# A three-block network on one core: the third block's tail on 516 tokens in two halves of 258 columns, each laid at 192 modulo 256 bytes

## The reference

```
def third_block(x, meta_tokens, ...):
    h = concatenate([meta, x], axis=1)                  # 16 + 512 tokens
    h = h + hybrid_mixer(rms_norm(h, norm_mix_w), w_in, ...)
    h = h + conv_ffn_3(rms_norm(h, norm_ffn_w), ffn_w_up, conv_w, conv_b, ffn_w_down)
    return rms_norm(h, norm_final_w)[:, N_META:]

def hybrid_mixer(h, ...):
    proj = h @ w_in
    fox_qkv, fox_f, gdn_qkv, gdn_z, gdn_b, gdn_a, gates = split(proj)
    o_fox = forgetting_attention(...)                   # looks back over all tokens
    gdn_qkv = silu(causal_dwconv(gdn_qkv, gdn_conv_w))  # width 4
    o_gdn = gated_delta_rule(...)                       # a scan over all tokens
    o_gdn = rms_norm(o_gdn, gdn_norm_w) * silu(gdn_z)
    return (g_fox * (o_fox @ w_branch_fox) + g_gdn * (o_gdn @ w_branch_gdn)) @ w_out

def conv_ffn_3(h, ...):
    u = causal_dwconv(h @ w_up, conv_w, conv_b)         # width 3: needs two tokens ahead
    gate, up = u[..., :2816], u[..., 2816:]
    return (silu(gate) * up) @ w_down
```

## Time and profile before

| what | value |
|---|---|
| median of 3 runs | 2911.84 us (2908.43 to 2922.6) |
| profiled execution | 2912.08 us, of which the span is 2910.7 us |
| mean granted TensorE clock | 0.975 |
| PE, DVE, ACT, POOL busy | 95%, 55%, 36%, 21% |
| stages behind the scans | about 2278 to 2911 us of the span |

### The profile page before, as it was taken

One profiled execution on the slowest core, in us unless ns is written; L12 is line 12 of the kernel. 1 busy time (PEld: TensorE's weight loads), 2 busy tenths in 40 slices (PEclk: granted clock), 3 DMA queues, 4 the chain that ended last, 5 costly groups with the idle time before them and its releaser, 6 DMA issues. The chain is left out here.

```text
span 2910.7 us, 42543 instructions
## 1 busy us (share of the span) xinstructions
PE 2778.8 (95%) x16646; PEld 2344.9 (81%) x16646; DVE 1604.3 (55%) x2432; ACT 1047.3 (36%) x1786; POOL 616.8 (21%) x495
## 2 busy tenths in 40 slices
PE   8989999999999999999999999999898998999998
PEld 6769876888888767757788888976787998999986
DVE  5875566366643475934533337964443455666643
ACT  4354343432223323252423224546343333422223
POOL 3430110121100222440100003445453000111101
PEclk9999899999999999989999999998999999999999
DMA  4200321123233312202232222210000122222221
GB/s 158 91 6 8 102 87 59 58 90 99 94 97 99 111 61 74 87 10 85 90 100 94 94 96 72 89 37 1 6 2 1 59 88 80 80 92 91 87 97 63
DMA packets 60307, 210.62 MB, mean 72 GB/s; under 512 B 7926, under 2 KB 8566, under 8 KB 59990
## 3 DMA queue, kind: packets, MB, share of 16 engines
q1 hardware_dynamic: 58934, 207.39, 21.8%
q10 hardware_dynamic: 1184, 0.59, 0.1%
HBM read 205.84 MB, written 2.10 MB: 71 GB/s over the span
## 5 line engine op out<-in xcount | busy, mean ns | idle before, releaser
L278 PE MATMUL ps<-normed,slab_hi 128*128 128x264 f32 (+2 forms) x2568 | 871.0, 339 | 27.4 <-DVE normed L601 13.8
L280 PE MATMUL ps<-normed,slab_lo 128*128 128x264 f32 (+2 forms) x2568 | 849.0, 331 | 0.0
L279 PE MATMUL ps<-normed,slab_hi 128*128 128x264 f32 (+2 forms) x2568 | 847.9, 330 | 0.0
L159 ACT ACTIVATE slab_hi<-ring 128x1024 fp32r<-128x1024 f32 x376 | 397.0, 1057 | 953.9 <-PE ps L280 949.6
L163 DVE TENSOR_TENSOR slab_lo<-ring,slab_hi 128x1024 fp32r<-128x1024 f32 x360 | 480.2, 1336 | 381.1 <-ACT slab_hi L159 380.6
L278 PEld LDWEIGHTS ps<-normed,slab_hi 128*128 128x128 f32 x2568 | 485.3, 189 | 89.4 <-issue 33.8
L279 PEld LDWEIGHTS ps<-normed,slab_hi 128*128 128x128 f32 x2568 | 488.1, 190 | 47.0 <-issue 4.3
L280 PEld LDWEIGHTS ps<-normed,slab_lo 128*128 128x128 f32 x2568 | 485.3, 189 | 46.6
L278 PE MATMUL ps<-hidden,slab_hi 128*128 128x512 f32 x560 | 221.9, 396 | 5.6 <-DVE hidden L229 5.6
L280 PE MATMUL ps<-hidden,slab_lo 128*128 128x512 f32 x560 | 220.1, 393 | 0.0
L279 PE MATMUL ps<-hidden,slab_hi 128*128 128x512 f32 x560 | 219.4, 392 | 0.0
(11 more groups left out here) (579 smaller groups left out, 3942.1 us busy)
## 6 DMA issues: line engine op xcount, KB each, us to landing
ring<-in_stream SPq DMA_DIRECT2D x376, 512.0 KB, 3.3
h<-in_x SPq DMA_DIRECT2D x8, 256.0 KB, 5.5
mix_y<-in_sgu_b SPq DMA_DIRECT2D x1, 1024.0 KB, 6.1
out_features<-ffn_hidden SPq DMA_DIRECT2D x2, 512.0 KB, 3.2
xn<-in_c_recip_count SPq DMA_DIRECT2D x1, 512.0 KB, 3.4
rwkv_a<-in_mem SPq DMA_DIRECT2D x1, 512.0 KB, 3.9
rwkv_b<-in_mem SPq DMA_DIRECT2D x1, 512.0 KB, 5.0
sgu_ln<-in_sgu_ln SPq DMA_DIRECT2D x1, 512.0 KB, 6.8
```

The costliest lines, as they stand in the source:

```text
L159: self.nc.scalar.activation(self.hi[:, n % PARTS, :], self.ring[:, n % SLOTS, :], ACT.Copy).then_inc(self.hi_ready, 1)
L278: nc.tensor.matmul(to, lhsT[0], rhs[0], start=start, stop=False)
L279: nc.tensor.matmul(to, lhsT[0], rhs[1], start=False, stop=False)
L280: return nc.tensor.matmul(to, lhsT[1], rhs[0], start=False, stop=stop)
```

## The change

It has four parts. Nothing is computed otherwise than before; tokens 0 to 11 are no longer carried behind the scans.

1. Behind the scans the stages work on tokens 12 to 527 (`FROM = META - 4`, `TAIL = 516`), in two halves of 258 columns: gates, z, the norm of `yg`, the merge, the output projection, the norm of the feed-forward and its up-projection. The projections before the scans keep 528.
2. Moving operands of these stages are laid by halves: each half of a row has a space of `HALF = 320` words (1280 bytes, a multiple of 256) of its own, and begins at 192 modulo 256 bytes. `Rows` has a flag `apart` and `Rows.moving` for it, and the splits write a row as two pieces of 258.
3. The projections' rows (`CarriedRows`) are contiguous: 528 words are 2112 bytes, so the first row begins at 160 (`CARRIED_AT`), the next 64 bytes further modulo 256, and each second half 32 bytes beyond its first.
4. The feed-forward's buffer `ffn3_raw` is the norm's `square` buffer. The down-projection's operands still begin at 192.

The order of the instructions and their number stay the same on every engine; their sizes change. The diff, cut to its core (left out: the same change of `0:T3` to `FROM:T3` in the activations of the gates, `HALVES` to `TAIL_HALVES` in the merge and the output, and the shift of the convolution's columns by 12):

```diff
+FROM = META - 4
+TAIL = T3 - FROM
+TAIL_HALVES = [(FROM, FROM + TAIL // 2), (FROM + TAIL // 2, T3)]
...
-OPERAND_AT = 192
-WIDE_AT, WIDE = 224, 576
-HIDDEN_AT = (OPERAND_AT - WIDE_AT) % BOUNDARY // 4
+OPERAND_AT, CARRIED_AT = 192, 160
+HALF = 320
...
-        self.hi, self.lo = at or K.moving(ctx, "rows", [parts] + shape)
+        self.hi, self.lo = at or K.moving(ctx, "rows", [parts] + shape, HALF if len(shape) == 3 else 0)
...
     def slab(self, i):
...
-    def moving(self, ctx, name, shape):
-        at, pitch = (OPERAND_AT, shape[-1]) if shape[-1] <= S else (WIDE_AT, WIDE)
+    def moving(self, ctx, name, shape, pitch=0, at=OPERAND_AT):
+        pitch = pitch or shape[-1]
...
 def laid(space, shape, pitch):
...
-    return rows if len(shape) == 2 else rows.rearrange("p (a b) n -> p a b n", b=shape[1])
+    if len(shape) == 3:
+        return rows.rearrange("p (a b) n -> p a b n", b=shape[1])
+    return rows if len(shape) == 2 else rows.rearrange("p (a b c) n -> p a b c n", b=shape[1], c=shape[2])
...
 def load_stage(K, ins):
...
-    def __init__(self, K, ctx, gain, n, scale=None, known=False, arrived=None, src=None, like=None):
+    def __init__(self, K, ctx, gain, n, scale=None, known=False, arrived=None, src=None, like=None, apart=False, at=OPERAND_AT):
...
-            self.square, self.total, self.rstd = like.square, like.total, like.rstd
+            self.square, self.total, self.rstd, self.apart = like.square, like.total, like.rstd, like.apart
...
-        self.hi, self.lo = K.moving(ctx, "normed", [KT, n])
+        self.apart = apart
+        self.hi, self.lo = K.moving(ctx, "normed", [KT, 2, n // 2], HALF) if apart else K.moving(ctx, "normed", [KT, n], at=at)
...
+    def moving(self, k, c, lo, hi):
+        return [x[:, k, c] if self.apart else x[:, k, lo:hi] for x in (self.hi, self.lo)]
+    def shaped(self, x):
+        return x.rearrange("p (c n) -> p c n", c=2) if self.apart else x
     def split_hi(self, act, k):
...
-        self.K.nc.scalar.activation(self.hi[:, k], self.src(k), ACT.Copy, scale=self.K.vec(self.gain, k)).then_inc(self.hi_ready, 1)
+        self.K.nc.scalar.activation(self.hi[:, k], self.shaped(self.src(k)), ACT.Copy, scale=self.K.vec(self.gain, k)).then_inc(self.hi_ready, 1)
...
     def split_lo(self, dve, k):
...
-        self.K.nc.vector.scalar_tensor_tensor(out=self.lo[:, k], in0=self.src(k), scalar=self.K.vec(self.gain, k),
+        self.K.nc.vector.scalar_tensor_tensor(out=self.lo[:, k], in0=self.shaped(self.src(k)), scalar=self.K.vec(self.gain, k),
...
     def take_square(self, act, k):
...
     def __init__(self, K, ctx, scale, gains):
-        super().__init__(K, ctx, "norm_mix_w_3", T3, scale)
+        super().__init__(K, ctx, "norm_mix_w_3", T3, scale, at=CARRIED_AT)
...
-                           (rows.hi[:, k, lo:hi], rows.lo[:, k, lo:hi]), k == 0, k == KT - 1)
+                           rows.moving(k, c, lo, hi), k == 0, k == KT - 1)
...
 def half_product(K, feed):
...
     def product(i, b, start, stop):
-        lo, hi = HALVES[b % 2]
...
-            mm = exact(K.nc, K.ps[:, b, 0:hi - lo], cut(feed.slab(i), at, at + P), [x[:, k, lo:hi] for x in feed.acts(i)],
+            mm = exact(K.nc, K.ps[:, b, 0:TAIL // 2], cut(feed.slab(i), at, at + P), [x[:, k, b % 2] for x in feed.acts(i)],
...
-def pairs_of(x):
-    n = x.shape[1] // 2
-    return lambda i: x[:, 2 * (i % n):2 * (i % n) + 2, :]
+def tail_pair(x, i):
+    return x[:, 2 * i:2 * i + 2, FROM:T3].rearrange("p k (c n) -> p k c n", c=2)
...
 class Rates:
...
-        rows = Rows(K, local, "norm_mix_w_3", T3, scale, known=True)
+        rows = Rows(K, local, "norm_mix_w_3", TAIL, scale[:, FROM:T3], known=True, src=lambda k: K.h[:, k, FROM:T3], apart=True)
...
-        raw = K.buf(local, "gates3_raw", [P, 2, T3])
-        root = K.buf(local, "gdn_root_mean", [P, 4, T3])
+        raw = K.buf(local, "gates3_raw", [P, 2, TAIL])
+        root = K.buf(local, "gdn_root_mean", [P, 4, TAIL])
...
-                        nc.vector.tensor_scalar(cols.grid(root[:, t, :]), K.ps[:, 6:8, 0:T3 // 2], 1.0 / HD, EPS, ALU.mult, ALU.add).then_inc(mean_out, 1)
+                        nc.vector.tensor_scalar(cols.grid(root[:, t, :]), K.ps[:, 6:8, 0:TAIL // 2], 1.0 / HD, EPS, ALU.mult, ALU.add).then_inc(mean_out, 1)
...
-                    nc.gpsimd.tensor_tensor(root[:, t, :], yg[:, t, :], yg[:, t, :], ALU.mult).then_inc(squared, 1)
+                    nc.gpsimd.tensor_tensor(root[:, t, :], yg[:, t, FROM:T3], yg[:, t, FROM:T3], ALU.mult).then_inc(squared, 1)
...
-                    nc.gpsimd.tensor_tensor(yg[:, t, :], yg[:, t, :], z[:, t, :], ALU.mult)
+                    nc.gpsimd.tensor_tensor(yg[:, t, FROM:T3], yg[:, t, FROM:T3], z[:, t, FROM:T3], ALU.mult)
...
-        part = K.buf(local, "merge3_part", [P, 2, 8, T3 // 2])
-        feed = Feed(K, local, 8, lambda i: (yf, yg)[(i // 2) % 2][:, 2 * (i % 2):2 * (i % 2) + 2, :], [2, T3])
+        part = K.buf(local, "merge3_part", [P, 2, 8, TAIL // 2])
+        feed = Feed(K, local, 8, lambda i: tail_pair((yf, yg)[(i // 2) % 2], i % 2), [2, 2, TAIL // 2])
...
-            (lo, hi), at = HALVES[b % 2], merged(4 * (g // 2) + b // 2)
+            (lo, hi), at = TAIL_HALVES[b % 2], merged(4 * (g // 2) + b // 2)
...
     def __init__(self, K, x, then, parts):
...
-        self.feed = Feed(K, None, 8, pairs_of(x), [2, T3], parts=PARTS, at=parts)
+        self.feed = Feed(K, None, 8, lambda i: tail_pair(x, i % 4), [2, 2, TAIL // 2], parts=PARTS, at=parts)
...
-        spaces = K.spaces(local, "rows", WIDE_AT, PARTS * 2 * WIDE)
-        out3 = Residual3(K, K.xn, rows, [laid(x, [PARTS, 2, T3], WIDE) for x in spaces])
-        ffn = Ffn(K, local, "ffn3", rows, 2 * FT, FT, [laid(x, [PARTS, HIDDEN_AT + S], 2 * WIDE)[:, :, HIDDEN_AT:] for x in spaces])
-        raw = K.buf(local, "ffn3_raw", [P, 2, T3])
+        spaces = K.spaces(local, "rows", OPERAND_AT, PARTS * 4 * HALF)
+        out3 = Residual3(K, K.xn, rows, [laid(x, [PARTS, 2, 2, TAIL // 2], HALF) for x in spaces])
+        ffn = Ffn(K, local, "ffn3", rows, 2 * FT, FT, [laid(x, [PARTS, S], 4 * HALF) for x in spaces])
+        raw = rows.square
...
-                    link(nc.vector.tensor_scalar(to, x[:, META - 2:T3 - 2], K.vec("ffn_conv_w_3", w), K.vec("ffn_conv_b_3", w), ALU.mult, ALU.add))
+                    link(nc.vector.tensor_scalar(to, x[:, 2:2 + S], K.vec("ffn_conv_w_3", w), K.vec("ffn_conv_b_3", w), ALU.mult, ALU.add))
...
-        rows = Rows(K, span, "norm_ffn_w_3", T3)
+        rows = Rows(K, span, "norm_ffn_w_3", TAIL, src=lambda k: K.h[:, k, FROM:T3], apart=True)
```

More of the change, by code:

```diff
@@ L3372, in _ @@
                     if i < 4:
-                        nc.scalar.activation(z[:, i, :], raw[:, i % 2, :], ACT.Silu).then_inc(gated, 1)
+                        nc.scalar.activation(z[:, i, FROM:T3], raw[:, i % 2, :], ACT.Silu).then_inc(gated, 1)
                     else:
-                        nc.scalar.activation(gates[:, i - 4, :], raw[:, i % 2, :], ACT.Sigmoid, bias=K.vec("gate_bias_3", i - 4)).then_inc(gated, 1)
+                        nc.scalar.activation(gates[:, i - 4, FROM:T3], raw[:, i % 2, :], ACT.Sigmoid, bias=K.vec("gate_bias_3", i - 4)).then_inc(gated, 1)
                     if i == SUMS + 4:
@@ L3397, in _ @@
                         dve.wait_ge(inverted, i - APPLY + 1)
-                        at = yg[:, t, lo:hi]
+                        at = yg[:, t, FROM + lo:FROM + hi]
                         nc.vector.scalar_tensor_tensor(out=at, in0=at, scalar=gain, in1=root[:, t, lo:hi], op0=ALU.mult, op1=ALU.mult).then_inc(normed, 1)
@@ L3896, in _ @@
                     for b in range(8):
-                        (lo, hi), m = HALVES[b % 2], 4 * (g // 2) + b // 2
+                        (lo, hi), m = TAIL_HALVES[b % 2], 4 * (g // 2) + b // 2
                         group.bank_ready(dve, b)
@@ L3955, in vector @@
             for b in range(8):
-                (lo, hi), m = HALVES[b % 2], 4 * g + b // 2
+                (lo, hi), m = TAIL_HALVES[b % 2], 4 * g + b // 2
                 group.bank_ready(dve, b)
@@ L4101, in _ @@
                         dve.wait_ge(multiplied if o else silu, f - 1)
-                    link(nc.vector.tensor_scalar(to, x[:, META - 2:T3 - 2], K.vec("ffn_conv_w_3", w), K.vec("ffn_conv_b_3", w), ALU.mult, ALU.add))
-                    link(nc.vector.scalar_tensor_tensor(out=to, in0=x[:, META - 1:T3 - 1], scalar=K.vec("ffn_conv_w_3", 2 * FT + w), in1=to, op0=ALU.mult, op1=ALU.add))
-                    nc.vector.scalar_tensor_tensor(out=to, in0=x[:, META:T3], scalar=K.vec("ffn_conv_w_3", 4 * FT + w), in1=to, op0=ALU.mult, op1=ALU.add).then_inc(conv, 1)
+                    link(nc.vector.tensor_scalar(to, x[:, 2:2 + S], K.vec("ffn_conv_w_3", w), K.vec("ffn_conv_b_3", w), ALU.mult, ALU.add))
+                    link(nc.vector.scalar_tensor_tensor(out=to, in0=x[:, 3:3 + S], scalar=K.vec("ffn_conv_w_3", 2 * FT + w), in1=to, op0=ALU.mult, op1=ALU.add))
```

(1 more changed line is left out.)

## The result

The changed kernel took 2894.24 us (median of 8 runs, 2887.86 to 2901.94) against 2914.36 us before (8 runs): a ratio of 0.9919, 95% interval 0.9903 to 0.9934 (the two medians alone give 0.9931). The medians are 20.1 us apart; the interval is 19 to 28 us. The forecast was 15.0 us.

What follows compares the result with a forecast made beforehand. Behind the scans TensorE (PE) sets the pace: matmul count times step. Terms -13.2 - 2.5 + 1.0 - 0.3 = -15.0 us took 2911.8 to 2896.8 us, range 2891 to 2908.

Steps and rivals of the forecast that it cites:

- (1): Gates and feed-forward, 3072 matmuls: step falls from 123.3 to 119.0 ns, 13.2 us saved.
- (2): Merge and output projection, 768 matmuls: step falls from 122.2 to 119.0 ns, 2.5 us saved.
- The line: Step by columns through the 256- and 512-column operands starting at 192: 118.1 ns plus 0.432 per column over 256.
- the high end: Upper bound of the 258-column step, today's less the columns' 2.5 ns: 120.8 in (1), 119.7 in (2); 9.6 us saved.
- (3): Projections, 1200 matmuls, contiguous rows through all eight starts: 1.0 us lost; bounds 2.0 us saved to 4.0 us lost.
- (4): Other engines work on 516 for 528 columns: 0.3 us off PE's four waits, the rest hidden; two-piece rows cost nothing.
- (5): Feed-forward buffer ffn3_raw shared with the norm's squares: no new wait arises.
- (6): Half-clock stretches behind waits: 258 columns save 5 ns on some 30 matmuls, counted as nothing.
- B: Rival: only the columns count, 9.6 us saved in (1) and (2), nothing in (3), 2902 us; chance 0.22.
- C: Rival: the row's end at 200 matters, 258 columns cost like 264, kernel takes 2908 to 2916 us; chance 0.13.
- D: Rival: same place as C but dearer, step 130.3 ns, 28 us lost, 2940 us; chance 0.05.
- E: Rival: PE's short half-clock stretches after waits, one more or less costs or saves 2 us in every case; no chance given.

Runs made afterwards that it cites:

- e2: Kernel before with only tokens 12 to 527 (258 columns) behind the scans, all operands lying as before: 2913.46 us, ratio 0.9978.
- e3: Kernel before with contiguous projection rows, gates' low parts 512 bytes further, feed-forward pitch 640 words: steps 120.7 (projections), 123.2 (gates), 123.3 ns (up-projection).
- e12: The changed kernel itself, unchanged, measured again: 2898.56 us, ratio 0.9925 to the kernel before; up-projection step 122.2 ns.
- e15: Changed kernel with 264 columns, projections as before, halves at 128 (gates), 64 (merge), 96 (output), 32 (feed-forward): steps 121.2, 120.1, 120.0, 121.7 ns.
- e8: Changed kernel with weight slabs starting at 64 for 128; 512-column, gates and feed-forward operands at 128, merge 192, output 0: 229.1, 118.6, 118.6, 122.1, mostly 120.8 ns.
- e1: Kernel before, still 264 columns, with each half behind the scans starting at 192 modulo 256, projections as before: 2905.62 us, ratio 0.9965.
- e13: Changed kernel with contiguous merge and feed-forward rows from 160, gates and projections at pitch 544 words: steps 119.7 (up-projection), 120.1 (gates), 121.0 ns (projections).
- e14: Changed kernel with gates' halves at 160 and 192, merge's at 64 and 96, feed-forward pitch 592 words, projections contiguous from 128: up-projection 119.7, gates 119.1 ns.
- e7: Changed kernel with most gates matmuls cut to 234 columns and most up-projection ones to 210, output not the reference's: steps 111.9 and 111.4 ns.

## Why the forecast fell short

(1) and (2), 258 columns at 192: right in size, and a little too careful. The line had 119.0 ns, the trace 118.6; against 123.3 that is 3072 x 4.7 = 14.4 us for the 13.2 of the sum, and 768 x 3.6 = 2.8 us for 2.5. Choosing the low end of its bounds was right: the high end, 120.8, is about what the columns give alone (121.1 in e2). Two things in it were luck. One of its reasons, that merge and output are nearer to the line because fewer of their matmuls change the start, doesn't hold: start to start the merge of before has 123.3 ns like the gates (the 122.6 came of dividing a short stretch by its count less one), and only its output was lower, by a rhythm that e3 with the same starts doesn't show. And the feed-forward took its fast rhythm in the profile behind this comparison; in e12 it did not, which takes back 7 of the 14.4 us.

(3), the projections' rows, is the step that failed, and in its sign. It took 1.0 us lost; by the steps 1200 x 2.5 = 3.0 us were gained, beyond the 2.0 us that its bound allowed. The stage itself became only 1.6 us shorter in this profile, since it spent more time at half clock there; here are before, after, and e15, which has the rows of before and the clock of after and takes 2.8 us more than after:

```profile
1758.60:1927.40 168.80, 164.57 (x1292) 0.99 0.25 79
1768.00:1935.20 167.20, 162.97 (x1293) 0.98 0.25 80
1763.60:1933.60 170.00, 165.81 (x1292) 0.98 0.24 79
```

Three choices made it. It took 192 for the best start and everything else for about as bad as what was there, while 224 and 0 are the dearest pair: any mixture had to be cheaper. And it priced the others by the only row with a start at 128, whose stationary operand also lay elsewhere; e8 shows that the difference of both starts counts, so that row said nothing on 128 (at 264 columns it has 121.2 in e15). Third, its best case priced 192 at 264 columns by the line, 121.6 ns, where e1 measured 120.9; so even the bound of 2.0 us was too low, by 0.8. Why contiguous rows are as cheap as 120.8 is explained for 1.7 of their 2.5 ns and open for the other 0.8 (e13, e14, e15).

(4) and (5) held: the waits are the same four, nothing new came, L232 and L228 are shorter by 2%; of the 0.3 us the waits show 0.1 (11.9 us for 12.0). That a row in two pieces costs nothing was assumed, and came out so. (6), at half clock, is small enough to say nothing either way.

With (3) put right and (1) and (2) as measured by their steps the sum is 14.4 + 2.8 + 3.0 + 0.3 = 20.5 us, 0.9930; both measured ratios, 0.9919 and 0.9925, hold it in their intervals. Because the forecast of 15.0 us stood on the border of what can be told from no change, I gave no difference as much chance as a gain; the 4 us by which (3) was wrong, with 1.5 us of (1) and (2), made it a clear gain.

The rivals: B (columns alone) fell with e1, where places alone bring 2.4 ns. C and D (a row that ends at 200 costs more) fell with the 118.6 ns. E, the clock, was real and larger than the 2 us I allowed: 9.4 us in the part of the profiled execution that nothing had touched. No rival had a stage with two rhythms.

## To carry to other kernels

Where three matmuls per product stream without a wait, the start of the moving operand against that of the stationary one, modulo 256 bytes, moved the step here by up to 3.5 ns of 120 (and 6.6 of 229): measure which difference is cheap, here 64 bytes, and move either side to it. It makes the fast rhythm possible and not certain, so look at more than one profile. Cut columns down to where the step meets its floor (111 ns, by the estimate above about 240 columns, here), and not further. Read such a change by its steps over long stretches, stage by stage; the total time of one execution moved by 9 us here for reasons of its own.

## What was not expected of the hardware

- The places of the moving and the stationary operand act together. With both moved by 64 bytes the steps of gates, feed-forward and 512 columns stayed (118.6 and 229.1 ns); with one moved they changed by 1.3 to 4.4 ns. The Trainium skill (TensorE: Matmul & The Clock Gate, Step-by-step: what each phase is for) has two independent read ports and says that loading the next weights takes no read bandwidth from the running matmul; the steps here depend on both starts all the same, and whether that happens at the reads no run shows. The Trainium skill's gap for a matmul by itself (TensorE: Matmul & The Clock Gate, Back-to-back issue gap), N / 2.4 + 2.5 ns, makes an estimate of 112.5 ns at 264 columns and 215.8 at 512, and the same section has a sustained 131 ns at 512; the best measured here are 120.0 and 228.9.
- Starts that differ by 8 bytes can act in opposite ways for different lengths: 200 against 192 is -0.4 to -0.9 ns at 258 columns and +6.6 at 512.
- One program has two steady rhythms in one stage, 118.6 and 122.2 ns, and kept the slower one for over 220 us. Steps of a single profile are to be taken with that in mind. At 192 and 258 columns the three profiles of the changed kernel have 118.7 to 119.1 in gates, merge, output and feed-forward, with one exception in twelve (e12); e7's merge and the end of the output in e7, e13 and e14 had 122.2 as well. At 192 and 512 columns the down-projection had 228.9 in nine profiles and 233.3 in three.
- What fixes these numbers inside the chip is open; nothing here shows it.
